# Experts' low halves of the sixth and the fourteenth weight piece on GpSimd, the other 22 on VectorE

## The reference

```python
def swiglu(h, w1, w3, w2):
    return jnp.matmul(jax.nn.silu(jnp.matmul(h, w1)) * jnp.matmul(h, w3), w2)

def moe_swiglu(h, router, w1, w3, w2):
    logits = jnp.einsum('bld,de->ble', h, router, preferred_element_type=F32)
    top_v, top_i = lax.top_k(logits, TOP_K)          # TOP_K = 2 of N_EXPERTS = 8
    wts = jax.nn.softmax(top_v, axis=-1)
    gates = jnp.sum(jax.nn.one_hot(top_i, N_EXPERTS, dtype=F32) * wts[..., None], axis=-2)
    y = jnp.zeros_like(h)
    for e in range(N_EXPERTS):
        y = y + gates[..., e:e + 1].astype(h.dtype) * swiglu(h, w1[e], w3[e], w2[e])
    return y
```

## Time and profile before

| | us |
|---|---|
| median of 3 runs | 1910.73 (1908.95 to 1914.78) |
| the profiled execution's own time | 1910.98 |
| its span, first to last instruction | 1909.2 |
| PE busy | 1780.1 (93%) |
| DVE busy | 1167.7 (61%) |
| ACT busy | 370.3 (19%) |
| POOL busy | 83.1 (4%) |
| line 1882, 192 instructions on DVE | 582.6 |

### The profile page before, as it was taken

One profiled execution on the slowest core, in us unless ns is written; L12 is line 12 of the kernel. 1 busy time (PEld: TensorE's weight loads), 2 busy tenths in 40 slices (PEclk: granted clock), 3 DMA queues, 4 the chain that ended last, 5 costly groups with the idle time before them and its releaser, 6 DMA issues.

```text
span 1909.2 us, 33853 instructions
## 1 busy us (share of the span) xinstructions
PE 1780.1 (93%) x14871; PEld 1124.5 (59%) x14871; DVE 1167.7 (61%) x1389; ACT 370.3 (19%) x667; POOL 83.1 (4%) x74
## 2 busy tenths in 40 slices
PE   6999999987799999999999967799999999999998
PEld 2334556664344444445556635497887968778795
DVE  1121166874523232323233594799999999999998
ACT  2001155222422222112013423201000100100010
POOL 0032000010000000000230001000000000000000
PEclk9999999998899999999999998899999999999999
DMA  9731200001345444311212104499999999999995
GB/s 351 303 132 66 89 1 14 32 1 65 143 185 224 181 163 184 134 67 44 88 67 88 44 1 164 154 408 405 419 414 419 416 417 418 404 410 404 419 416 207
DMA packets 98777, 408.70 MB, mean 214 GB/s; under 512 B 13944, under 2 KB 20792, under 8 KB 84304
## 3 DMA queue, kind: packets, MB, share of 16 engines
q1 hardware_dynamic: 96440, 405.54, 53.9%
q10 hardware_dynamic: 2200, 1.08, 0.2%
HBM read 405.55 MB, written 1.05 MB: 213 GB/s over the span
## 4 chain that ended last, share of the span: by engine, by line
PE 74%; DVE 11%; DMA 6%; issue 3%; ACT 1%; SPq 1%; PEld 1%; DVEq 1%; POOL 1%; POOLq 0%; PEldq 0%; ACTq 0%
PE PS L1425 12%; PE PS L1786 11%; PE PS L688 9%; PE PS L686 8%; PE PS L1385 6%; DMA ARENA<-in_moe_w 4%; PE PS L1764 4%; PE PS L1766 4%; PE PS L1767 4%; PE PS L1320 3%; DVE ARENA L1882 3%; PE PS L451 2%; PE PS L1213 2%; DMA ARENA<-in_ada_w 2%; DVE ARENA L880 1%
## 5 line engine op out<-in xcount | busy, mean ns | idle before, releaser
L1882 DVE TENSOR_TENSOR ARENA<-ARENA 128x2816 bf16<-128x2816 f32 (+1 forms) x192 | 582.6, 3084 | 12.5 <-DMA ARENA<-in_moe_w 11.2
L1764 PE MATMUL PS<-ARENA 128*128 128x96 bf16 x2816 | 382.7, 210 | 13.7 <-DVE ARENA L1882 11.8
L1767 PE MATMUL PS<-ARENA 128*128 128x96 bf16 x2816 | 382.3, 207 | 2.0 <-issue 2.0
L1766 PE MATMUL PS<-ARENA 128*128 128x96 bf16 x2816 | 382.4, 209 | 0.9 <-issue 0.9
L1766 PEld LDWEIGHTS PS<-ARENA 128*128 128x128 bf16 x2816 | 355.7, 126 | 6.9 <-issue 6.2
L1764 PEld LDWEIGHTS PS<-ARENA 128*128 128x128 bf16 x2816 | 347.2, 123 | 19.6 <-DVE ARENA L1882 13.2
L1767 PEld LDWEIGHTS PS<-ARENA 128*128 128x128 bf16 x2816 | 299.8, 106 | 2.6 <-issue 2.6
L688 PE MATMUL PS<-ARENA 128*128 128x512 f32 (+1 forms) x608 | 243.8, 541 | 2.2 <-DVE ARENA L604 2.2
L1786 PE MATMUL PS<-ARENA 128*96 128x512 bf16 x1056 | 237.5, 384 | 0.7 <-DVE ARENA L1882 0.6
L1425 PE MATMUL PS<-ARENA 128*128 128x512 bf16 x1056 | 232.8, 381 | 2.4 <-DVE ARENA L1456 2.4
L1786 PEld LDWEIGHTS PS<-ARENA 128*96 128x96 bf16 x1056 | 128.0, 122 | 103.6 <-issue 1.3
(11 more groups left out here) (238 smaller groups left out, 1640.7 us busy)
## 6 DMA issues: line engine op xcount, KB each, us to landing
ARENA<-in_moe_w SPq DMA_DIRECT2D x128, 1408.0 KB, 15.2
ARENA<-in_moe_w SPq DMA_DIRECT2D x48, 1536.0 KB, 18.2
ARENA<-in_ada_w SPq DMA_DIRECT2D x24, 2048.0 KB, 10.3
ARENA<-in_ffn_w SPq DMA_DIRECT2D x15, 2048.0 KB, 7.7
ARENA<-in_w_in SPq DMA_DIRECT2D x11, 2048.0 KB, 7.9
ARENA<-in_moe_w SPq DMA_DIRECT2D x16, 1024.0 KB, 17.5
ARENA<-in_w_out SPq DMA_DIRECT2D x8, 1024.0 KB, 5.5
ARENA<-in_w_in SPq DMA_DIRECT2D x6, 1024.0 KB, 8.3
```

The source lines that it names most:

```text
L1764: pe.matmul(out, hi[:, h][:, f], HEH[:, k, :], start=k == 0 and b % 4 == 0, stop=False, skip_group_check=True)
L1766: pe.matmul(out, hi[:, h][:, f], HEL[:, k, :], start=False, stop=False, skip_group_check=True)
L1767: mm = pe.matmul(out, lo[:, h][:, f], HEH[:, k, :], start=False, stop=k == KC - 1, skip_group_check=True)
L1882: dve.tensor_tensor(WLO[q % NSLOT][:, 0:n], RAW[q % NSLOT][:, 0:n], WHI[q % NSLOT][:, 0:n], ALU.subtract).then_inc(S("m_lo"), 1)
```

## The change

A new function `pool_moe` puts the subtraction of q = 5 and q = 13 on POOL, once per expert, with the same operands and after the same landing semaphore; it raises a semaphore of its own, `m_lo_pool`. DVE skips these two pieces. PE waits for `m_lo_pool` before these two, and for `m_lo`, counted to 22 per expert, before the others.

```diff
+        POOL_PIECES = (5, 13)
+
+        def lo_done(pe, i, q):
+
+            if q in POOL_PIECES:
+                pe.wait_ge(S("m_lo_pool"), 2 * i + POOL_PIECES.index(q) + 1)
+            else:
+                pe.wait_ge(S("m_lo"), 22 * i + q + 1 - sum(p < q for p in POOL_PIECES))
+
+        def pool_moe(pool):
+
+            def body(i, e):
+                for q in POOL_PIECES:
+                    n = piece_words(q)
+                    pool.wait_ge(S(f"m_raw{q % NSLOT}"), 16 * (3 * i + q // NSLOT + 1))
+                    pool.tensor_tensor(WLO[q % NSLOT][:, 0:n], RAW[q % NSLOT][:, 0:n], WHI[q % NSLOT][:, 0:n],
+                                       ALU.subtract).then_inc(S("m_lo_pool"), 1)
+            rounds(pool, body)
...
         def pe_moe(pe):
             def uv_piece(i, q, bank0):
 
-                pe.wait_ge(S("m_lo"), NPIECE * i + q + 1)
+                lo_done(pe, i, q)
...
             def y_piece(i, q):
-                pe.wait_ge(S("m_lo"), NPIECE * i + q + 1)
+                lo_done(pe, i, q)
...
         def dve_moe(dve):
             def body(i, e):
                 for q in range(NPIECE):
+                    if q in POOL_PIECES:
+                        continue
                     n = piece_words(q)
...
                 pool_norm(pool, 2 * L + 1)
                 stage_end(pool, "pool")
+            pool_moe(pool)
```

## The result

The changed kernel takes 1917.9 us (median of 16 runs, 1913.77 to 1927.13), the kernel before 1909.62 us in its 16 runs beside it. The ratio is 1.0047, 95% interval 1.0034 to 1.0060: slower by 6.5 to 11.5 us. The profiled execution took 1917.85 us, its span is 1916.0. One execution of e14_twice took 9437.65 us and is left out of its ratio.

The account below looks back on a forecast made before the run. DVE, with PE and transfers also full, was to set the pace: 75.7 + 2 x 6.4 - 0.3 = 88.2 us per expert, 4.8 over 83.4, x 8 = 38.4 on 1910.98, giving 1949.4 us; likeliest 1935 to 1967, 8-in-10 range 1907 to 1972.

Parts of the forecast that it names:

- What bounds the kernel: In the experts DVE, PE and transfers are all full; relieving DVE returns at most PE's 6.6 us of waits.
- The disputed term: POOL's SBUF-reading subtraction blocks DVE's instructions with two SBUF operands for its whole length, 6.4 us each.
- the term for the two holds: DVE's blocked time per expert from POOL's two subtractions: 2 x 6.4 us, less 0.3 of cover.
- what POOL's subtraction takes: POOL's time for one 2816-word piece, extrapolated from shorter layer 0 instructions: 6.4 us, range 5.5 to 8.
- cover: DVE work possible during POOL's subtractions, instructions reading PSUM and only one SBUF operand: 0.3 us per expert.
- The slack: DVE needs 81.7 of the mean 83.4 us per expert: 1.7 us of slack, 14 us over eight.
- excess x 8: DVE's 88.2 us per expert exceeds 83.4 by 4.8, paid in all eight experts: 38.4 us.
- Marks: Expected profile signs: DVE's mean subtraction 3.7 us, DMA share 0.95, expert period near 88, PE waits some 40 us.
- first hold delays PE by 4 or 5 us: In the first expert, POOL's early piece 5 delays PE's start directly, by up to 4 or 5 us.
- It takes its turn at the next boundary: POOL gets in between DVE instructions that follow without a gap, read from one case at 428.08 us.
- the rows called additions: Layer 0 POOL rows on float32 operands, 1.35 us for 512 words, 1.07 for 384, used to estimate POOL's time.
- the third rival: Worse than forecast: POOL takes 8 us or more (1975), or no turn in DVE's run (up to 2040); chance 0.10.

Follow-up runs that it names:

- e14_twice: As the changed kernel, but POOL makes each of its two subtractions twice, with a wait between; 1995.44 us, ratio 1.0437 to the kernel before.
- e1_no_pool: Changed kernel without POOL's work: low halves of pieces 5 and 13 left out, DVE makes 22; 1910.12 us, ratio 0.9995 to the kernel before.
- the zero-fill: Changed kernel, but POOL subtracts 8 words of pieces 5 and 13 and writes zeros to the rest; 1912.01 us, ratio 1.0011 to the kernel before.
- e10: As the changed kernel, but POOL subtracts the float32 word from itself, so both operands are float32; 1917.88 us, ratio 1.0037 to the kernel before.
- e12: As the changed kernel, but POOL's piece 5 also waits for DVE's first subtraction of the same expert; 1918.08 us, ratio 1.0038 to the kernel before.
- e15: As the changed kernel, but POOL adds the high half instead of subtracting it; 1917.51 us, ratio 1.0040 to the kernel before.

## Why the prediction was wrong in size

- **What bounds the kernel**: right that DVE, PE and the transfers are full together and that relief brings little; e1_no_pool shows it brings at most 0.17%.
- **The disputed term** was right: POOL's reading and DVE's instruction with two SBUF operands exclude each other, for POOL's whole length, in both directions. DVE's longest subtraction (7.77 us) and line 1885 (5.12) show it, and the zero-fill, which reads nothing, leaves DVE alone where the two overlap. The rule quoted from the Trainium skill holds here in both directions.
- **The step that failed is the term for the two holds, and in it first what POOL's subtraction takes.** I extrapolated 6.4 us from instructions of 384 and 512 words, over five times shorter; it is 4.88, outside even the 5.5 to 8 that I left for it. The two holds cost DVE 8.4 us per expert, against 12.5 in the sum (2 x 6.4 - 0.3): 4.1 us per expert, 33 of the 38.4 us. Of that, 3.0 per expert are POOL's length. The other 1.1 are cover, 1.4 in place of my 0.3: a hold is shorter by what DVE does or waits for meanwhile, most of all at piece 13, whose landing falls on the hidden values in nearly each expert. The length alone would have put the forecast at 1925 us (75.7 + 9.8 - 0.3 = 85.2, 1.8 x 8 = 14 us more).
- **The slack** was too small: I took the mean period, 83.4 us, for what the transfers need. It holds the first expert, whose early pieces had landed before; after it they need 84.3 us, as e1_no_pool shows with DVE idle. With 84.1 us for DVE the change ends just under that edge, so the step "excess x 8" has nothing to multiply. What is left is paid once: DVE, 99.6% busy, no longer catches up with the landings and is 4.2 us further behind when the last piece has landed. The runs e10, e12 and e15, with the same holds, repeat a loss of 0.37 to 0.40%, and in their traces 24.1 to 26.5 us lie behind the last landing, in the changed kernel 24.3, before 19.5 and in e1_no_pool 19.1.
- **Marks**: DVE's mean rose to 3.29 us, not 3.7; the DMA share stayed at 1.01; I named both as marks of the size, and both told it.
- The smaller part "first hold delays PE by 4 or 5 us" was 2.7, and e12_late_first shows no gain from taking it away.
- Two readings and a sum were off without deciding anything. "It takes its turn at the next boundary" was read from one case; of the seven boundaries ahead of DVE's piece 6 after the first expert, six had no gap, and POOL won one of them and lost five. Of the rows called additions, line 829 is a multiplication, and both are slower than POOL's subtraction in the experts. And the third rival's upper end, 1949.4 plus 16 x 6.4, is 2052 and not 2040.
- Not settled: the trace holds 4.7 us of the loss in the experts, while the runs give 6.5 to 11.5 us. From DVE's first subtraction to the end, e10, e12 and e15 take 688.2 to 689.4 us, 5.8 to 7.0 more than before, which reaches the interval's lower end; there is one trace of the kernel before, and where the rest lies is open. Why DVE's distance from the landings stays at 6 to 7 us in the changed kernel, and does not shrink slowly, was not tested either.

## What to carry to other kernels

Moving work from DVE to POOL does not put it beside DVE's work when POOL's instruction reads SBUF and DVE's have two SBUF operands: the sum of both is what must fit, here 3.3 to 4.7 us of hold against 3.0 of relief. Where DVE reads PSUM the hold was shortest, and still more than the relief. An excess within DVE's slack costs nothing while the transfers set the pace, but DVE must have caught up when the last of them lands. Before pricing a move, ask what the relief is worth by leaving the work out; and never take a duration from instructions five times shorter when the whole sum rests on its product with sixteen, without giving its lower end the weight of its upper.

## What the hardware showed that was not expected

- POOL does not always get its turn: in e14_twice it waited 12.3 us through a gapless run of DVE's subtractions and then ran at once. Its record in the profile holds that wait, so a long POOL instruction (15.2 us) is not long work (4.88).
- POOL's two-operand instruction ran at 1.67 ns a word from 256 to 2816 words in the experts, and slower (1.27 us instead of 1.03 for 512) in layer 0.
- A hold behind the boundary costs less than POOL's length: 4.69 us at most of 4.88 when a subtraction was next, and 3.3 to 4.5 on line 1885, behind the instructions that read PSUM.
